# Seven products of halves for 16 of the 22 inner blocks of the down projections

## The reference

```
def _swiglu(h, wg, wu, wd):
    a = jnp.einsum('btd,df->btf', h, wg)
    b = jnp.einsum('btd,df->btf', h, wu)
    return jnp.einsum('btf,fd->btd', jax.nn.silu(a) * b, wd)

xp = xp + g2p[:, None] * _swiglu(hp, ...)    # prompt tokens, gate g2p
xs = xs + g2s[:, None] * _swiglu(hs, ...)    # sample tokens, gate g2s
```

## Time and profile before

| | |
|---|---|
| median of 3 runs | 3023.31 us |
| the profiled execution | 3026.01 us |
| its span, first to last instruction | 3024.1 us |
| mean granted clock of TensorE | 0.979 |
| TensorE matmuls | 2881.4 us, 95% |
| VectorE | 1603.4 us, 53% |
| GpSimd | 1400.6 us, 46% |
| ScalarE | 940.6 us, 31% |

### The profile page before, as it was taken

The page is one execution under the profiler, slowest core; times in us unless marked ns, Lnnn a source line. Parts: engine busy times, 40 slices in busy tenths (PEclk is TensorE's granted clock), DMA queues, the critical chain, the costliest instruction groups (busy, mean ns, idle before and its releaser), DMA issues. The chain is left out here.

```text
span 3024.1 us, 59642 instructions
## 1 busy us (share of the span) xinstructions
PE 2881.4 (95%) x24697; PEld 2678.1 (89%) x24697; DVE 1603.4 (53%) x2968; ACT 940.6 (31%) x1988; POOL 1400.6 (46%) x1273
## 2 busy tenths in 40 slices
PE   6999999996789999999999999999999999999998
PEld 4859999765689999999999999956699999999998
DVE  6399999556646644444345500066648544334435
ACT  3351111355533433332101311166525333332001
POOL 2122224463533877776334233144334777775333
PEclk9999999998899999999999999999999999999999
DMA  6726763642251122223322223163221221224222
GB/s 217 250 73 223 253 222 124 185 146 70 96 183 47 61 78 78 85 81 126 106 80 69 77 90 114 42 214 111 77 90 40 82 81 69 85 78 150 79 76 74
DMA packets 179181, 338.76 MB, mean 112 GB/s; under 512 B 21064, under 2 KB 94560, under 8 KB 177056
## 3 DMA queue, kind: packets, MB, share of 16 engines
q1 hardware_dynamic: 138576, 281.64, 27.4%
q10 hardware_dynamic: 40336, 53.31, 4.9%
HBM read 268.30 MB, written 79.49 MB: 115 GB/s over the span
## 5 line engine op out<-in xcount | busy, mean ns | idle before, releaser
L109 PE MATMUL tr_acc<-tr_quad_hi,ah_ring_hi 128*128 128x264 f32 x2432 | 694.5, 286 | 8.4 <-DVE tr_kept L1190 2.2
L111 PE MATMUL tr_acc<-tr_quad_hi,ah_ring_lo 128*128 128x264 f32 x2432 | 692.7, 285 | 0.0
L110 PE MATMUL tr_acc<-tr_quad_lo,ah_ring_hi 128*128 128x264 f32 x2432 | 690.2, 284 | 0.0
L577 POOL TENSOR_TENSOR ah_ring_lo<-ah_raw,ah_ring_hi 128x512 fp32r<-128x512 f32 (+1 forms) x402 | 554.8, 1386 | 159.1 <-ACT ah_ring_hi L920 146.2
L109 PEld LDWEIGHTS tr_acc<-tr_quad_hi,ah_ring_hi 128*128 128x128 f32 x2432 | 458.6, 189 | 10.6 <-DVE tr_kept L1190 2.6
L110 PEld LDWEIGHTS tr_acc<-tr_quad_lo,ah_ring_hi 128*128 128x128 f32 x2432 | 458.7, 189 | 0.1
L111 PEld LDWEIGHTS tr_acc<-tr_quad_hi,ah_ring_lo 128*128 128x128 f32 x2432 | 458.2, 188 | 0.0
L575 POOL CAST ah_ring_hi<-ah_raw 128x512 fp32r<-128x512 f32 (+1 forms) x162 | 102.9, 635 | 528.9 <-PE tr_acc L111 464.6
L109 PE MATMUL tr_acc<-tr_part_hi,ah_ring_hi 128*128 128x352 f32 x1038 | 335.6, 323 | 2.0 <-DVE tr_kept L1228 2.0
L110 PE MATMUL tr_acc<-tr_part_lo,ah_ring_hi 128*128 128x352 f32 x1038 | 332.9, 321 | 0.0
L111 PE MATMUL tr_acc<-tr_part_hi,ah_ring_lo 128*128 128x352 f32 x1038 | 332.6, 320 | 0.0
(11 more groups left out here) (391 smaller groups left out, 6418.8 us busy)
## 6 DMA issues: line engine op xcount, KB each, us to landing
f_ada_w<-in_w_ada_dram SPq DMA_DIRECT2D x48, 1024.0 KB, 5.6
scratch_inner<-tr_kept ACTq DMA_DIRECT2D x88, 264.0 KB, 2.2
tr_staged<-scratch_inner SPq DMA_DIRECT2D x44, 528.0 KB, 4.3
ah_raw<-in_w_gate_dram SPq DMA_DIRECT2D x44, 512.0 KB, 3.5
ah_raw<-in_w_up_dram SPq DMA_DIRECT2D x44, 512.0 KB, 4.5
ah_raw<-in_w_down_dram SPq DMA_DIRECT2D x64, 256.0 KB, 3.6
f_raw<-in_w_dram SPq DMA_DIRECT2D x24, 512.0 KB, 7.5
out_z_dram<-f_stage ACTq DMA_DIRECT2D x60, 176.0 KB, 1.9
```

What stands on the lines that cost most here:

```text
L109: pe.matmul(out, w_hi, hi, start=start, stop=False)
L110: pe.matmul(out, w_hi, lo, start=False, stop=False)
L111: return pe.matmul(out, w_lo, hi, start=False, stop=stop)
L577: pool.tensor_tensor(lo[:, 0:width], own, hi[:, 0:width].bitcast(F32), ALU.subtract).then_inc(w_ready, 1)
```

## The change

The inner blocks are cut as 3, 4, 4, 4, 4, 3. Parts 0 and 5 stay in the form of before. In parts 1 to 4 each unit, a product of [2 x 2 halves of weights] with [2 x 2 halves of the operand], is made by seven products of halves instead of eight. The halves are two output blocks, two by two inner blocks, and two column halves; the right half is prompt columns 496 to 1023, the left half the others with the samples.

- **TensorE**: 7 products, each 2 column blocks x 2 inner blocks x 3 = 12 matmuls of 264 columns. M1, M6, M7, M4 are summed in one PSUM pair one after the other, M5 and M3 in a second, M2 in a third. The order is M1, M5, M6, M3, M2, M7, M4, where M4 comes behind M1 and M5 of the next unit.
- **VectorE** reads the PSUM pair after each product and adds gate times it to x (seven reads of 528 columns; for three of them the sample columns are an instruction of their own). It makes the mixtures of the operand (M5, M6, M4) and all lower halves, each in two instructions of 528 columns, one behind each of 20 products of the part before. For part 1 they stand two by two behind the steps of part 0; for parts 3 and 4 they begin six products later than for part 2.
- **ScalarE** casts the upper halves of the operand, seven of 1056 columns per part, and the upper halves of the weight factors, seven of 256 columns per unit.
- **GpSimd** makes the M7 operand (two of 528 columns per part), four mixtures of 256 columns and seven lower halves of 256 columns per unit.
- **SyncE** loads the four quarters of a part in ten transfers (the left ones in four each: runs of 248 and of 16 elements). They stand ahead of the weights of units 2 (part 1), 3 and 5 (part 2), 9 (part 3), 13 (part 4) and 17 (part 5, three transfers). The loads for parts 3, 4 and 5 wait until the part two before has been used up by TensorE.
- The raw, upper and lower operand share one place per quarter: the lower half is written over the raw one.

```diff
-TRUNK_PARTS = [4, 4, 4, 4, 3, 3]
+TRUNK_PARTS = [3, 4, 4, 4, 4, 3]
 assert sum(TRUNK_PARTS) == KF
 PART_FIRST = [sum(TRUNK_PARTS[:p]) for p in range(len(TRUNK_PARTS))]
 PART_MAX = max(TRUNK_PARTS)
+SEVENTHS = (1, 2, 3, 4)
+PLAIN_PARTS = [p for p in range(len(TRUNK_PARTS)) if p not in SEVENTHS]
...
+DOWN_ORDER = [M1, M5, M6, M3, M2, M7, M4]
...
+            if u in self.split_no:
+                run = [v for v in range(u, end) if all(w in self.split_no for w in range(u, v + 1))]
+                for v in run:
+                    for n, product in enumerate(DOWN_ORDER[:6]):
+                        if n == 2 and v > u:
+                            self.events += [("product", v - 1, M4), ("read", v - 1, M4)]
+                            order.append((v - 1, M4))
+                        self.events += [("product", v, product), ("read", v, product)]
+                        order.append((v, product))
+                self.events += [("product", run[-1], M4), ("read", run[-1], M4)]
+                order.append((run[-1], M4))
+                u = run[-1] + 1
...
+            elif e == "product":
+                self.bank[u, t] = {M5: 1, M3: 1, M2: 2}.get(t, 3 * (self.split_no[u] % 2))
+                self.free_after[u, t] = held.get(self.bank[u, t])
+            elif e == "read":
+                adds += 1
+                self.read_no[u, t] = adds
+                held[self.bank[u, t]] = ("x", adds)
...
-        staged = at("staged", [P, PART_MAX, N], F32, 8 * QUAD)
-        part_hi = [at(f"part{g}_hi", [P, PART_MAX, N], F32R, h * QUAD) for g, h in enumerate((0, 4, 10))]
-        part_lo = [at(f"part{g}_lo", [P, PART_MAX, N], F32R, h * QUAD) for g, h in enumerate((2, 6, 12))]
+        part_homes = {0: (0, 8 * QUAD), 5: (11 * QUAD, 11 * QUAD + 3 * EIGHTH * 4)}
+        part_hi = {p: at(f"part{p}_hi", [P, TRUNK_PARTS[p], N], F32R, part_homes[p][0]) for p in PLAIN_PARTS}
+        part_raw = {p: at(f"part{p}_raw", [P, TRUNK_PARTS[p], N], F32, part_homes[p][1]) for p in PLAIN_PARTS}
+        part_lo = {p: at(f"part{p}_lo", [P, TRUNK_PARTS[p], N], F32R, part_homes[p][1]) for p in PLAIN_PARTS}
+        odd_home = dict(zip(DOWN_ORDER, (4, 5, 6, 7, 11, 12, 13)))
+        even_home = {M1: 2, M7: 3, M3: 10, M5: 0, M6: 1, M2: 8, M4: 9}
+        seventh_homes = {1: odd_home, 2: even_home, 3: odd_home, 4: even_home}
...
+        rest_items = [("mix", M5, 0), ("mix", M5, 1), ("mix", M6, 0), ("mix", M6, 1), ("rest", M1, 0), ("rest", M1, 1),
+                      ("mix", M4, 0), ("mix", M4, 1)] + [("rest", q, h) for q in DOWN_ORDER[1:] for h in range(2)]
+        upper_after, rest_after = {}, {}
+        for p in range(len(TRUNK_PARTS) - 1):
+            host = [at for what, *at in events if what in ("mm", "product") and (at[0] - DOWN_FIRST) // 4 == p
+                    and DOWN_FIRST <= at[0] < plan.z_first]
+            if p + 1 in SEVENTHS:
+                if p in SEVENTHS:
+                    late = 0 if p == 1 else 6
+                    where = [2 + late + i for i in range(20)]
+                    uppers = [late + i for i in (4, 6, 8, 10, 12, 15, 17)]
+                else:
+                    where = [2 + p // 2 + i * (10 - p // 2) // 20 for i in range(20)]
+                    uppers = [2 + p // 2 + i for i in range(7)]
+                for i, item in enumerate(rest_items):
+                    rest_after.setdefault(tuple(host[where[i]]), []).append((p + 1, item))
+                for i, q in enumerate(DOWN_ORDER):
+                    upper_after.setdefault(tuple(host[uppers[i]]), []).append((p + 1, q))
...
+        def part_over(eng, p):
+
+            u = DOWN_FIRST + 4 * p + 3
+            if p in SEVENTHS:
+                eng.wait_ge(product_done, plan.product_no[u, M4] + 1)
             else:
-                eng.wait_ge(step_done, plan.last_step[DOWN_FIRST + 4 * (p - 3) + 3] + 1)
+                eng.wait_ge(step_done, plan.last_step[u] + 1)
+
+        def place_free(eng, p, early=False):
+
+            if p == 0:
+                eng.wait_ge(made[1], 7 * (KF // 2 - 2) + 2)
+            elif p == 1:
+                eng.wait_ge(made[1], 7 * (KF // 2 - 1))
+            elif p == 2 and early:
+                eng.wait_ge(made[1], 7 * (KF // 2 - 1))
+            elif p < 5:
+                part_over(eng, p - 2)
+            else:
+                part_over(eng, 3)
...
+            def left_load(p, q, kh):
+                for k in range(2):
+                    f = PART_FIRST[p] + 2 * kh + k
+                    stored_inner(f)
+                    dst = eighth_raw[p, q][:, k].rearrange("p (b n) -> p b n", b=2)
+                    sp.dma_start(dst[:, :, 0:LEFT_TOKENS], io["inner"][f][:, 0:LEFT].rearrange("p (b n) -> p b n", b=2)
+                                 ).then_inc(eighth_in[p, q], 16)
+                    sp.dma_start(dst[:, :, LEFT_TOKENS:BLOCK], io["inner"][f][:, T:N].rearrange("p (b n) -> p b n", b=2)
+                                 ).then_inc(eighth_in[p, q], 16)
+
+            def right_load(p, q, kh):
+                f = PART_FIRST[p] + 2 * kh
+                stored_inner(f + 1)
+                sp.dma_start(eighth_raw[p, q][:], io["inner"][f:f + 2, :, LEFT:T].rearrange("k p n -> p k n")).then_inc(eighth_in[p, q], 16)
+
+            def eighth_loads(p, first, rest):
+                if first:
+                    place_free(sp, p, True)
+                    left_load(p, M1, 0)
+                    right_load(p, M7, 0)
+                    right_load(p, M3, 1)
+                if rest:
+                    place_free(sp, p)
+                    left_load(p, M2, 1)
...
+                if u == DOWN_FIRST + 1:
+                    part_loads(0)
+                elif u == DOWN_FIRST + 2:
+                    eighth_loads(1, True, True)
+                elif u == DOWN_FIRST + 3:
+                    eighth_loads(2, True, False)
+                elif u == DOWN_FIRST + 5:
+                    eighth_loads(2, False, True)
+                elif u == DOWN_FIRST + 9:
+                    eighth_loads(3, True, True)
+                elif u == DOWN_FIRST + 13:
+                    eighth_loads(4, True, True)
+                elif u == DOWN_FIRST + 17:
+                    part_loads(5)
...
+            def seventh_factor(u, n):
+                v, b = plan.split_no[u], u % 2
+                r11, r12, r21, r22 = (down_factor(u, DOWN_ORDER.index(q)) for q in (M1, M2, M7, M4))
+                mix = w_sum[b][:, 0:2 * P]
+                if n == 0:
+                    loaded(pool, u)
+                split(u, n, down_factor(u, n))
+                if n == 0:
+                    if v >= 2:
+                        pool.wait_ge(w_ready, plan.slot_no[plan.split_units[v - 2], DOWN_ORDER.index(M3)] + 1 - AHEAD)
+                    pool.tensor_tensor(mix, r21, r22, ALU.add).then_inc(factor_mix, 1)
+                    pool.wait_ge(factor_mix, 4 * v + 1)
+                    pool.tensor_tensor(r21, r11, r21, ALU.subtract).then_inc(factor_mix, 1)
+                elif n == 1:
+                    pool.wait_ge(w_ready, plan.slot_no[u, 1] + 1 - AHEAD)
+                    pool.wait_ge(factor_mix, 4 * v + 2)
+                    pool.tensor_tensor(r11, mix, r11, ALU.subtract).then_inc(factor_mix, 1)
+                    pool.wait_ge(factor_mix, 4 * v + 3)
+                    pool.tensor_tensor(mix, r12, r11, ALU.subtract).then_inc(factor_mix, 1)
+                    pool.wait_ge(factor_mix, 4 * v + 4)
+
+            def mix_seventh(p):
+                place_free(pool, p, True)
+                eighth_landed(pool, p, M3)
+                for h in range(2):
+                    mixed(pool, p, M5, h)
+                    own = eighth_raw[p, M7][:, h]
+                    pool.tensor_tensor(own, eighth_raw[p, M3][:, h], own, ALU.subtract).then_inc(eighth_mix7, 1)
...
+            def seventh(u, product):
+                p, n = seventh_of(u), DOWN_ORDER.index(product)
+                bank_free(u, product)
+                weights_ready(pe, plan.slot_no[u, n])
+                if units[u][1] == 0:
+                    pe.wait_ge(eighth_ready, 14 * place_no(p) + 2 * n + 2)
+                w_hi_s, w_lo_s = slot(u, n)
+                out, fresh = pair[plan.bank[u, product]], product in (M1, M2, M5)
+                for b in range(2):
+                    for k in range(2):
+                        of = slice(P * k, P * k + P)
+                        upper, lower = (v[p, product][:, k, BLOCK * b:BLOCK * b + BLOCK] for v in (eighth_hi, eighth_lo))
+                        done = passes(pe, out[:, b, 0:BLOCK], w_hi_s[:, of], w_lo_s[:, of], upper, lower, fresh and k == 0, k == 1, not fresh)
+                done.then_inc(product_done, 1)
...
+                if u in plan.split_no:
+                    v, product = plan.split_no[u], DOWN_ORDER[to]
+                    if product in (M1, M2, M4):
+                        loaded(act, u)
+                    else:
```

(20 more changed lines are left out.)

253 lines of the change are left out of this document (181 added, 72 removed).

## The result

The changed kernel takes **3074.32 us** (median of 4 runs, 3068.98 to 3074.70). Beside it on the same chip the kernel before took 3023.97 us. The ratio is 1.0164, with a 95% interval of 1.0141 to 1.0187: 50 us slower. I had forecast 3042, and slower. The sign was right, but the time lies above my range. The profiled execution has a span of 3072.3 us against 3024.1, 48.2 us more. From the first to the last matmul of the down stage it is 25.6 us longer in layer 0 and 25.7 in layer 1.

The account below looks back on a forecast made before the run. TensorE's matmuls were taken to bound both down stages. The terms -39.7 + 2 x (11.1 + 17.1) + 2.4 = +19 us gave 3042 us on the median's scale; the forecast's own range was 3026 to 3062, the wider one 2998 to 3068.

Parts of the forecast that it names:

- the landing of the weights at the boundaries: Weights queued behind part loads: unit 9's land 9.0 us after part 1 is over, unit 13 the same, unit 17's 7.2.
- "no wait" at unit 5: Only four transfers ahead: weights land at 4.8 us, M4 of unit 4 ready at 10.8, wanted at 11.7.
- VectorE at nothing: Parts 1 to 4: 1.45 us of VectorE per product against TensorE's 1.457, with 0.1 us of exclusion; no cost.
- TensorE's saving, 39.7 us: Inner blocks of parts 1 to 4: each unit takes 10.20 us for 11.44, saving 19.9 us per layer, 39.7 in all.
- Rival A: The gain comes through because loads land earlier or SyncE's order hurts little: 3001 us, or 2984 without waits; chance 0.23.
- The boundaries, 36.6 us with the clock: Late weights behind part loads: 6.3 us at unit 9, 6.3 at 13, 4.5 at 17, 17.1 per layer; clock 2.4.
- The chain of 6.0 us to M4: From the weights' landing, ScalarE's cast and GpSimd's factors make M4 of the preceding unit ready after 6.0 us.
- The clock, 2.4 us: TensorE's granted clock drops after idling at four boundaries: 0.6 us each, between 0 and 1.2, 2.4 in all.
- The stretches, 22.2 us: Units within parts 1 to 3: GpSimd's factor loop and M7 operand delay TensorE 3.7 us per part, 11.1 per layer.
- The 0.4 us per collision for GpSimd: In parts 1 to 3, each VectorE operation that excludes GpSimd costs GpSimd 0.4 us, between 0 and 0.55.
- rival C: VectorE bounds the stretches, waiting 0.4 us for GpSimd per operation: 1.75 us per product, 26 us more, 3068 us; chance 0.12.
- Rival B: Boundaries cost what was forecast, the factor loop nothing, because collisions fall into gaps: -3 us, 3020 us; chance 0.20.

Follow-up runs that it names:

- experiment 1: Changed kernel with the part loads of units 2, 3, 5, 9, 13 and 17 issued behind the weights: 3021.10 us, 0.9991 of the kernel before.
- experiment 3: Changed kernel with each left quarter loaded in two transfers with runs of 2112 bytes, not four (wrong column order): 3074.26 us, 1.0173 of the kernel before.
- experiment 4: Changed kernel with 54, 54 and 36 needless matmuls in TensorE's stalls ahead of M1 of units 9, 13 and 17: 3071.27 us, 1.0162.
- Experiment 6: Changed kernel with weights ahead of the part loads and GpSimd's M7 operand of parts 3 and 4 one unit later: 3021.12 us, 0.9993.
- experiment 2: Changed kernel with VectorE's 20 mixtures and lower halves per part replaced by one-source copies (output wrong): 3054.66 us, 1.0102 of the kernel before.
- experiment 5: Changed kernel with weights ahead of the part loads and VectorE's mixtures and lower halves replaced by one-source copies (output wrong): 3000.57 us, 0.9922.
- experiments 7 and 8: VectorE's and GpSimd's M7 pairs of 528 columns fused to 1056: 7 with weights first and later M7 operand, 3034.89 us; 8 on changed kernel alone, 3084.29 us.
- the best version: Changed kernel with weights ahead of part loads, M4 inside its unit, M7 operands moved and VectorE's operations spread: 3018.54 us, 0.9987.

## Why the prediction was wrong

Point by point, by its own steps. Three of them failed: the landing of the weights at the boundaries, "no wait" at unit 5, and VectorE at nothing.

**TensorE's saving, 39.7 us: right.** A product lasts 1.457 us wherever nothing is late, and with it the ledger gives the lengthening of the two down stages to 0.2 us. Rival A (the gain comes through) fell, since the waits are there.

**The boundaries, 36.6 us with the clock: the right mechanism, mis-sized.** They cost 50.7, and experiment 1 takes all of it away by the order of SyncE's queue alone. The step that failed is the landing "9.0 us after part 1 is over". It took 11.2 (1493.9 to 1505.1). Unit 13's weights landed 11.9 us after part 2 was over (9.0 forecast) and unit 17's 9.2 (7.2); in layer 1 it was 11.6, 11.2 and 8.7. The excess of the six is 13.4 us, for the 14.1 that were missed. The weights flew 5.6 us from their issue, not 2.9. The chain of 6.0 us to M4 held (1505.1 to 1511.1), though the text counts three free operations where its sum, and the timeline, have two.

The 9.0 came from the 299 GB/s of the window in the earlier trace rows, and a window tells what has moved, not what has landed. By the same trace the last of its four tiles landed 9.2 us after its issue, 10.6 after the burst began, and 0.54 of the window's 2.69 MB are the two stores. A later burst of the kernel before had the very case, four tiles and then 0.52 MB of weights (SyncE's issues, and the time of those two weight transfers to landing):

```profile
1432.17 1.79 SPq L531 DMA_DIRECT2D tr_staged<-scratch_inner  x4
```

```profile
1435.12 1.11 SPq L520 DMA_DIRECT2D ah_raw<-in_w_down_dram  x2
```

```profile
DMA to landing us min/median/max: 7.0/7.6/8.3
```

The second landed at 1443.8, 11.6 us after the burst began (11.6 in layer 1 too). That number, in place of 9.0, gives 8.9 us at units 9 and 13, where 8.9 to 9.9 were lost. The 5.4 us that ten issues took are not the reason: in experiment 3 the weights were issued 2.6 us earlier and landed no earlier at unit 9. What sets the rate stays open: in the 11.6 us of that earlier burst other loads moved besides, at 319 GB/s in all.

The Trainium skill ("DMA: Bandwidth & Descriptors", table of figures) says that runs below 512 bytes do not move at line rate, for which I had estimated 7 us. Experiment 3 shows no difference without the runs of 64 bytes. That does not contradict the page: in the trace one packet of 64 bytes keeps its DMA engine for 11 ns and one of 2048 bytes for 87, so per byte the short ones are four times slower. But 1024 of them over 16 engines are 0.7 us of engine time, and the engines were busy for 79% of the burst. The estimate was too high.

**The clock, 2.4 us: not told from nothing.** It fell to half, deeper than in the earlier trace rows, yet experiment 4 gives 3 us by the times and none in the boundaries of the ledger.

**The stretches, 22.2 us: too small.** They cost 34.3. The 0.4 us per collision for GpSimd was right: its operations of 256 columns have 1.09 to 1.20 us where they meet VectorE's, for 0.73 alone. Experiment 6 confirms what I said of the M7 operand, that the loop has no room for it wherever it stands. Two things were missing. One is unit 5, for which I had said "no wait": its weights landed 6.1 and 6.5 us after part 0 was over, not 4.8, and units 5 to 7 lose 8.4 us over both layers, 4 more than with the weights first. (With copies it is clearer: 7.2 us in experiment 2, 0.3 in 5.) The other is VectorE.

**"VectorE: I cost it at nothing" is the step that failed outright.** I charged 0.1 us of exclusion per operation, so that a product took 1.45 of 1.457 us. It is 0.43 by the median (1.12 less 0.69) and 0.32 in the mean, and a product with such an operation takes 0.72 + 0.63 + 0.43 = 1.78 us, or 1.67 in the mean. I had that case as rival C, at 0.12, and had argued against it that GpSimd's operations are half as long. The length of the one in the way is 0.73 us, and 0.44 to 0.56 of it is lost. This goes with the entry of part 1 (5.9 us in both layers in this execution, not foreseen at all: in part 0 two operations stand behind each step) and the 0.7 us at M2 of units 10, 11, 14 and 15. Experiment 2 puts VectorE's length and the collisions on both sides at 20 us together, where the forecast had only GpSimd's side of it.

Together: boundaries 14, unit 5 with its order 4, the rest of the stretches 8, entry 6, that is 32 us, the distance from 3042 to 3074. Rival B (boundaries only, 3020) had no stretch loss, which experiment 1 shows to be 13.7 and 15.5 us. Rival C gave 3068 us, near the time, but by 26 us in the stretches, where 12 were missed.

**How long one engine holds the other.** Behind an operation of 0.69 us GpSimd loses 0.35 to 0.47 us; behind one of 1.24 it loses 1.0. A fixed charge from one size does not carry to another, as experiments 7 and 8 show. What is constant is the end: in the traces of the changed kernel and of experiment 7, GpSimd's operation of 256 columns ends some 0.60 us after the end of the VectorE operation that was running when it started, so only 0.13 of its 0.73 us are hidden. It is the same 0.60 behind the copies of experiment 5. The other way round, in the four cases with no third operation, VectorE's 0.69 us end 0.57 us after GpSimd's end. The Trainium skill ("SBUF — State Buffer", Who interferes with whom) says that the first holds the ports for its whole instruction: by that rule, the trace agrees. I had misread and the earlier trace rows as speaking against it: L590 started 0.49 us before L1208's end and lost 0.35, the same 0.14 less. The rule costs what is left of the first operation when the second one starts, not its whole length, which is what I had priced.

**What stays open.** The 14.3 and 14.5 us that the best version still loses are VectorE's by the waits. Whether it is the length of its operations or the mutual waiting is not separated, since copies change both.

## What to carry to other kernels

Where a queue serves a ring with little cover (here six products, 8.7 us), order it by when each transfer is needed: putting the urgent 0.52 MB behind up to 2.16 MB of patient ones cost 53 us, more than the 39.7 that the change could win. For such a wait read the landing of the last transfer in a like burst, not the rate of a window. When a change shortens the bound engine's step, charge every collision to both engines, and sum each helper over the window in which it is full, the way in included. Keep a helper's pieces shorter than the slack of the read that stands behind them: fusing them saved collisions and lost 10 to 14 us.

## What the runs showed of the hardware

- A two-source operation of VectorE (528 columns, 0.69 us) and one of GpSimd (256 columns, 0.73 us) slow each other by 0.44 to 0.56 and 0.35 to 0.47 us. The one that comes second ends 0.57 us (VectorE) and 0.60 us (GpSimd) after the first's end. A VectorE copy with one source collides as well: 0.42 us alone, 0.8 to 1.0 in company, GpSimd 0.93.
- TensorE's granted clock was 0.89 in 5 us without a matmul, 0.50 (1.2 GHz) in the next 5 with 15 matmuls, and 0.93 in the 5 after. With needless matmuls in the gap it stayed at 1.00.
- 0.52 MB of weights behind 2.16 MB on the same queue landed 11.2 to 11.9 us after SyncE was free to issue with ten transfers ahead (issued in 5.4 us), and 10.6 to 11.5 with six (in 2.9 us).
- Four transfers with runs of 64 bytes beside six others cost nothing that could be measured: 3074.26 us without them, 3074.32 with them.
